# Two plain pairs instead of three at the head of each feed-forward part, and the token sums of two tiles moved ahead of the norm's root

## What is computed

```python
def _rmsnorm(x, g):
    r = xf * lax.rsqrt(jnp.mean(xf * xf, axis=-1, keepdims=True) + NORM_EPS)
    return r * g

def _swiglu(h, w_gate, w_up, w_down):
    return (jax.nn.silu(h @ w_gate) * (h @ w_up)) @ w_down

x = x + 1/2 * _swiglu(_rmsnorm(x, g), w_gate, w_up, w_down)     # D_FF = 2816
```

## Time and profile before

| | |
|---|---|
| median of 3 runs | 2819.61 us (2818.29 to 2819.61) |
| the profiled execution, its own time | 2818.11 us |
| its span, first to last instruction | 2815.9 us |
| TensorE busy | 2753.3 us, 98% |
| VectorE, ScalarE, GpSimd busy | 1442.4, 847.9, 1567.8 us |
| TensorE's mean granted clock | 0.993 |

### The profile page before, as it was taken

The page is one execution under the profiler, slowest core; times in us unless marked ns, Lnnn a source line. Parts: engine busy times, 40 slices in busy tenths (PEclk is TensorE's granted clock), DMA queues, the critical chain, the costliest instruction groups (busy, mean ns, idle before and its releaser), DMA issues.

```text
span 2815.9 us, 39727 instructions
## 1 busy us (share of the span) xinstructions
PE 2753.3 (98%) x14496; PEld 2306.6 (82%) x14496; DVE 1442.4 (51%) x1499; ACT 847.9 (30%) x1291; POOL 1567.8 (56%) x914
## 2 busy tenths in 40 slices
PE   7999999999999999999999999999999999999998
PEld 5888888888888888878988987887888888888886
DVE  7554554153556524027787866541447555553243
ACT  5333332132001112025656641111424333332222
POOL 3878775555454456645556554433044878774552
PEclk9999999999999999999999999999999999999999
DMA  3212224453222224322212113321021222224442
GB/s 134 105 67 89 89 82 157 156 210 127 105 89 97 105 98 154 125 91 71 55 35 56 50 52 127 114 78 42 0 97 68 93 79 89 73 84 174 176 157 104
DMA packets 125482, 278.36 MB, mean 99 GB/s; under 512 B 16592, under 2 KB 58704, under 8 KB 125160
## 3 DMA queue, kind: packets, MB, share of 16 engines
q1 hardware_dynamic: 103248, 215.67, 22.7%
q10 hardware_dynamic: 22168, 61.79, 5.8%
HBM read 215.46 MB, written 61.93 MB: 99 GB/s over the span
## 4 chain that ended last, share of the span: by engine, by line
PE 85%; issue 7%; POOL 4%; DVE 3%; ACT 1%; ACTq 0%; POOLq 0%; DVEq 0%
PE G L880 17%; PE G L881 17%; PE G L882 17%; PE G L964 9%; PE G L965 9%; PE G L966 9%; PE G L1222 2%; PE G L1391 1%; POOL AL L748 1%; PE G L1414 1%; PE G L1119 1%; PE G L1125 1%; DVE ylo L2562 0%; POOL rkb L723 0%; POOL Ys L708 0%
## 5 line engine op out<-in xcount | busy, mean ns | idle before, releaser
L806 POOL TENSOR_TENSOR whi<-raw,zero 128x1024 fp32r<-128x1024 f32 x129 | 249.5, 1934 | 826.1 <-PE G L882 784.2
L880 PE MATMUL G<-hhi,whi 128*128 128x512 f32 x1072 | 421.1, 393 | 17.4 <-DVE hlo L2032 17.4
L882 PE MATMUL G<-hhi,wlo 128*128 128x512 f32 x1072 | 418.6, 391 | 0.0
L881 PE MATMUL G<-hlo,whi 128*128 128x512 f32 x1072 | 418.6, 390 | 0.0
L809 POOL TENSOR_TENSOR wlo<-raw,whi 128x1024 fp32r<-128x1024 f32 x129 | 395.9, 3069 | 10.1
L2180 DVE TENSOR_TENSOR dl<-draw,dh 128x2048 fp32r<-128x2048 f32 x44 | 109.2, 2482 | 281.8 <-ACT dh L1639 281.8
L880 PEld LDWEIGHTS G<-hhi,whi 128*128 128x128 f32 x1072 | 202.0, 188 | 61.5 <-issue 15.4
L880 PE MATMUL G<-dh,whi 128*128 128x512 f32 x640 | 249.2, 389 | 0.0
L881 PE MATMUL G<-dl,whi 128*128 128x512 f32 x640 | 249.2, 389 | 0.0
L882 PE MATMUL G<-dh,wlo 128*128 128x512 f32 x640 | 249.2, 389 | 0.0
L882 PEld LDWEIGHTS G<-hhi,wlo 128*128 128x128 f32 x1072 | 202.0, 188 | 42.2
(11 more groups left out here) (443 smaller groups left out, 6507.1 us busy)
## 6 DMA issues: line engine op xcount, KB each, us to landing
draw<-a_d SPq DMA_DIRECT2D x44, 1024.0 KB, 5.8
a_d<-s SPq DMA_DIRECT2D x44, 512.0 KB, 3.0
raw<-in_wd SPq DMA_DIRECT2D x44, 512.0 KB, 3.5
raw<-in_wg SPq DMA_DIRECT2D x26, 512.0 KB, 3.9
raw<-in_wu SPq DMA_DIRECT2D x26, 512.0 KB, 4.8
raw_b<-in_wg SPq DMA_DIRECT2D x36, 256.0 KB, 3.4
raw_b<-in_wu SPq DMA_DIRECT2D x36, 256.0 KB, 4.1
x_park<-xT ACTq DMA_DIRECT2D x16, 512.0 KB, 2.6
```

The source lines that it names most:

```text
L806: nc.gpsimd.tensor_tensor(hi, raw[:, k, 0:w], zero[:].to_broadcast([P, w]), ALU.add).then_inc(hi_made, 1)
L880: nc.tensor.matmul(dst, wh, hi, start=start, stop=False)
L881: nc.tensor.matmul(dst, wh, lo, start=False, stop=False)
L882: return nc.tensor.matmul(dst, wl, hi, start=False, stop=stop)
```

## The change

`PLAIN` becomes 2 and `FAST` 20 in both feed-forward parts. VectorE's order becomes tile 0, tile 1, root, gate 0, tile 2, up 0, tile 3, gate 1, up 1. ScalarE's order becomes scale 0, scale 1, high 0, scale 2, high 1, scale 3, root, silu 0, high 2, weights' high parts 1 to 5 of fast pair 0, high 3, silu 1, high parts 6 and 7. The root's scratch (`nt_a`, `nms_a`) moves to a place that the token sums don't overwrite. As 20 is even, the peeled pair now stands in the loop's second place (`raw_b`, banks G2 and G3), the down product starts its tiles in the order 0 to 3, and one padding count of the bank semaphores goes.

```diff
-PLAIN = 3
+PLAIN = 2
 FAST = FFC - PLAIN
-PLAIN_AT = (1, 45)
+PLAIN_AT = (1, 43)
...
-    nt_a, nms_a = inside("x", 6 * ROW, "nt_a", [P, T]), inside("x", 7 * ROW, "nms_a", [P, T])
+    nt_a = nc.alloc_sbuf_tensor_at("nt_a", [P, T], F32, offset=sums_at - 12288)
+    nms_a = nc.alloc_sbuf_tensor_at("nms_a", [P, T], F32, offset=sums_at - 6144)
...
# SyncE
-            for u in range(2 * PLAIN - 1):
+            for u in range(2 * PLAIN):
                 plain(u)
+            sp.wait_ge(split_made, u0 + 2 * PLAIN + credit)
+            pair(0, 0)
             sp.wait_ge(dve_free, free + 1)
             store_a(0)
-            plain(2 * PLAIN - 1)
-            sp.wait_ge(split_made, u0 + 2 * PLAIN + credit)
-            pair(0, 0)
             sp.wait_ge(dve_free, free + 2)
             store_a(1)
             sp.wait_ge(unit_used, u0 + 2 * PLAIN + credit)
             pair(1, 1)
-            sp.wait_ge(dve_free, free + 3)
-            store_a(2)
...
# TensorE
-                    for o in (2, 3, 0, 1) if free is first_free else range(4):
+                    for o in range(4):
...
-            fast_pair(FAST - 1, 0, k, held[0])
-            c.advance(unit=2 * FAST, act=1, dve=1)
+            c.advance(unit=2 * FAST)
...
# ScalarE
         def ffn(own, gain, hi, nms, park=False):
-            norm_root(nms, nrf[:])
             k = c.unit % 2
             act.wait_ge(*nh_dve.at("l1", c.norm - 1))
...
             scale_tile(0, own)
-            plain_silu(0)
             scale_tile(1, own)
             tile_hi(0)
             scale_tile(2, own)
             tile_hi(1)
-            plain_silu(1)
             scale_tile(3, own)
+            norm_root(nms, nrf[:])
+            plain_silu(0)
             tile_hi(2)
-            tile_hi(3)
             c.advance(unit=2 * PLAIN)
             act.wait_ge(unit_used, c.unit - 1 + credit)
             for n in range(1, 6):
                 weight_hi(0, 0, n, k)
-            plain_silu(2)
+            tile_hi(3)
+            plain_silu(1)
             act.wait_ge(unit_used, c.unit + credit)
             for n in range(6, 8):
                 weight_hi(0, 0, n, k)
...
# VectorE
         def ffn(gain, hi, lo, nt, nms, nt_next, loads):
+            tile_sums(0)
+            tile_sums(1)
             norm_root(T, nms, nrf[:], nt)
             plain_gate(0)
-            tile_sums(0)
+            tile_sums(2)
             plain_up(0)
-            tile_sums(1)
+            tile_sums(3)
             plain_gate(1)
-            tile_sums(2)
             plain_up(1)
-            tile_sums(3)
-            plain_gate(2)
-            plain_up(2)
```

More of the change, by code:

```diff
@@ L599, in ffn_up @@
             pair(1, 1)
-            sp.wait_ge(dve_free, free + 3)
-            store_a(2)
-            with sp.Fori(1, FAST // 2) as i:
+            with sp.Fori(1, FAST // 2 - 1) as i:
                 for s in range(2):
@@ L607, in ffn_up @@
                     store_a(q + (PLAIN - 2))
-            pair(FAST - 1, 0)
+            pair(FAST - 2, 0)
+            sp.wait_ge(*st_dve.at("a1", c.fast + FAST - 4))
+            store_a(FAST - 4 + PLAIN)
+            pair(FAST - 1, 1)
             sp.wait_ge(a_out, (c.ffn * FFC + FFC - 3) * 16)
@@ L824, in _ @@
                         weight_sums(i * 2 + s, s, u0)
-                weight_sums(FAST - 1, 0, u0)
                 continue
@@ L1022, in first_free @@
             def first_free(o):
-                if o == 2:
+                if o == 0:
                     pe.wait_ge(*st_dve.at("c21", c.fast + FAST - 2))
-                elif o < 2:
-                    pe.wait_ge(*st_dve.at("c21" if o else "U3", c.fast + FAST - 1))
+                elif o >= 2:
+                    pe.wait_ge(*st_dve.at("c21" if o == 3 else "U3", c.fast + FAST - 1))
             def second_free(o):
@@ L1627, in ffn @@
                 weight_hi(0, 0, n, k)
-            c.advance(act=PLAIN + 1, dve=PLAIN + 1, a=PLAIN)
+            c.advance(act=PLAIN, dve=PLAIN, a=PLAIN)
             first = c.unit + 2 * FAST
@@ L1639, in down @@
                 activation(dh[v % 2][:], (draw[v % 2] if not isinstance(at, int) or at else draw0)[:], ACT.Copy).then_inc(*d_act.sig("hi"))
-            with act.Fori(0, FAST // 2) as i:
+            with act.Fori(0, FAST // 2 - 1) as i:
                 for s in range(2):
                     fast_pair(i * 2 + s, s, k)
-            fast_pair(FAST - 1, 0, k, False, down)
+            fast_pair(FAST - 2, 0, k)
+            fast_pair(FAST - 1, 1, k, False, down)
             c.advance(unit=2 * FAST)
@@ L2160, in ffn @@
             plain_gate(0)
-            tile_sums(0)
+            tile_sums(2)
             plain_up(0)
-            tile_sums(1)
+            tile_sums(3)
             plain_gate(1)
-            tile_sums(2)
             plain_up(1)
-            tile_sums(3)
-            plain_gate(2)
-            plain_up(2)
[L2170 to L2174, removed]
+            c.advance(unit=2 * PLAIN, act=PLAIN, dve=PLAIN, a=PLAIN)
             base = c.ffn * 2 * FFK
@@ L2180, in down @@
                 tt(dl[v % 2][:], src[:], dh[v % 2][:].bitcast(F32), ALU.subtract).then_inc(*d_dve.sig("lo"))
-            with dve.Fori(0, FAST // 2) as i:
+            with dve.Fori(0, FAST // 2 - 1) as i:
                 for s in range(2):
                     fast_pair(i * 2 + s, s)
-            fast_pair(FAST - 1, 0, lambda: down(0, 0))
+            fast_pair(FAST - 2, 0)
+            fast_pair(FAST - 1, 1, lambda: down(0, 0))
             c.advance(unit=2 * FAST)
```

## The result

The changed kernel takes 2838.96 us, median of 4 runs (2838.07 to 2839.65), against 2819.24 for the kernel before (2818.29 to 2819.61, 4 runs). The ratio is 1.0072, 95% interval [1.0056, 1.0088]: slower. The profiled execution's own time is 2838.07 us, its span 2835.7 us, 19.8 more than that of the kernel before. Here rows of the kernel after answer to those of before.

A forecast was written before the change was run, and what follows sets the result against it. TensorE, busy for 98% of the span, bounds the kernel, and loses whatever it waits for VectorE's chain. Heads and clock, 11.5 + 7.4 + 4 = +22.9 on 2818.1, give 2841; with 1.5 to the median, 2842 us (2827 to 2850).

The forecast's parts named there:

- Gain in matmuls: In each feed-forward part, a fast pair (19.3) replacing a plain pair (21.8) gains 2.5 us, plus 0.2 of waiting.
- First head: VectorE's chain to gate 1, counted with queueing behind GpSimd, starts fast pair 0 at 81.0; cost +11.5 us.
- Second head: The same chain count in the second head ends gate 1 at 2173.7; cost +7.4 us.
- That the root's operations queue: The root's three VectorE operations were assumed to wait behind GpSimd; if not, each head is some 2.4 us shorter.
- The clock: TensorE, idle for 10 us ahead of fast pair 0, then runs slower: 2 us per head, +4 in all, bounds 0 and 5.2.
- Edits at nothing: SP's later weight loads, the scratch's new place and the peeled last pair were costed at nothing.
- The count for SP and the late weights: In fast pair 0, block product 5's evacuation is done at about +14, and TensorE wants it at +13.8: level.
- The condition: If the slow clock's cover of 2 is gone, fast pair 1's late weights cost up to 1 us in each head.
- The sum: Both heads and the clock: 11.5 + 7.4 + 4 = +22.9 us on the profiled execution's 2818.1, giving 2841.
- Rival A: VectorE keeps up: fast pair 0 starts within 2.7 us of its natural time; at best 2814; chance 0.05.
- B: Queueing is half of that counted: fast pair 0 at 74 and 2169, +10.2 us, 2830; chance 0.15.
- C: Each tile costs what it did before: gate 1 ends at 83.7 and 2176.9, +29.8 us, 2849; chance 0.17.

The follow-up runs named there:

- e1: The kernel before, still with three plain pairs, given only the change's ScalarE and VectorE order and the scratch's new place; 2820.88 us.
- e4: The changed kernel with 28 idle matmuls into a free bank ahead of fast pair 0 in each head; 2840.45 us.
- e6: The changed kernel with the high parts of units 2 and 3 made by ScalarE in place of GpSimd in both heads; 2834.94 us.
- e5: The changed kernel with most of GpSimd's work in the first head cut to 32 columns, leaving out most of those weights' parts; 2826.26 us.
- e9: e5 with GpSimd's split of units 2 and 3 cut to 32 columns in the second head too; 2819.96 us.
- e3: The changed kernel with gate 1 evacuated ahead of tile 3's sums, up 1 behind them; 2845.61 us.
- e7: e3 with SP loading fast pair 1's weights ahead of the store of chunk 1; 2833.39 us.
- e8: The changed kernel with the edits of e6 and e7 together; 2831.44 us.

## Why the prediction was right

The forecast was 2842 (2827 to 2850), slower; the median is 2838.96. Step by step:

- **Gain in matmuls, 2.5 for each part.** The page has the 24 matmuls fewer, and a fast pair still takes 19.3 (85.92 to 105.23). Right.
- **First head.** Fast pair 0 at 81.0 was forecast and started at 80.79: +11.3 for +11.5. Within the chain, tile 0 ended at 41.8 (41.5), tile 1 at 50.9 (50.8), the root at 58.9 (60.4), tile 2 at 69.8 (70.4), up 0 at 73.3 (74.0), tile 3 at 79.4 (80.2). Only one of the root's three operations was held (2.17 where 1.23 is its pace), by 0.9 and not 2.3. Tile 2 made up half of that, 9.5 for the 8.8 counted. How many are held changes from trace to trace: one in e1 (2.80), two in e4 (2.22 and 2.17), none in e6. So agreement to a few tenths is in part luck. (The root's terms as written add up to 57.9 and not 58.1.)
- **Second head.** In before's time it started at 2184.46 - 10.35 = 2174.1, forecast 2173.7: +7.8 for +7.4. Here the root's first operation was held by the split of unit 3 for 2.1 (3.35).
- **That the root's operations queue** was the open bound. The runs show both sides: 3.35 beside a full split, 1.23 beside a narrow one (e5, e9).
- **The clock, 2 for each head.** From the first fast matmul to `s1c` it took 5.1 and 4.6 in place of 3.2 and 3.1 (the earlier trace rows and the rows of the second head above): 2.0 and 1.5. e4 measured the same 2.0 by removing it. The mechanism is shown, but that the size came out near 2 is in part luck: behind the long waits of e3 and e5 to e9 it was 1.4 to 2.5. Of the two rows that the 2 was taken from, the one at the kernel's start has 12 matmuls in 5.3 us, but a granted clock of 1.00; its 2.5 rests on the matmuls' pace alone.
- **Edits at nothing.** The count for SP and the late weights held: `s5c` came 13.8 after the first fast matmul (forecast 14), level with TensorE. The condition held too: where the slow clock was gone (e4, e5), it cost 1.0 to 1.1 (in e9's first head 0.5). The scratch and the peeled pair show no wait of their own in any of these profiles.
- **The sum.** Heads: 11.3 + 2.0 + 7.8 + 1.5 = 22.6 against 22.9. In the profile, the 2.9 by which the total is smaller is the middle. No trace shows why the median of the other runs is also 3 below the forecast; sixteen runs of the kernel before in a later session lie from 2812.75 to 2820.52, and I had no term for such scatter.

Rival A (VectorE keeps up) needed a GpSimd that isn't in the way. e5 is that case, and it only draws level in its head. B (half the queueing) is refuted by the first three tiles' 8.7, 9.1 and 9.5, and by 80.79 where it had 74. C (each tile as before) would have had gate 1 end at 83.7; it ended at 80.5. The queueing is told apart from both by e5 and e9: with GpSimd's operations cut and nothing taken from VectorE, the loss goes.

My reasons failed in the experiments. For e3 I had named the late weights in the prediction and then moved up 1 behind tile 3 without carrying the count through SP's queue, and I left out that gate 1 waits for the store of `s`. For e4 I did not count that the idle matmuls themselves start behind a rest. For e6 and e8 I took two GpSimd operations off the chain and left out that an earlier chain meets the next ones.

## What to carry to other kernels

Before taking covering work away from the engine that is the bound, write out the chain of the engine that was covered, with every operation of GpSimd that falls into it. An operation with two SBUF inputs is to be priced by what GpSimd does at that moment, not by its mean. When one wait is shortened, carry the count through to the next: the slow clock had hidden late weights, and the gate had hidden a store. To save 2.5 us of matmuls, a slack of the same size was all that this order had, and the chain missed it by 11.

## What the runs showed of the hardware

- GpSimd and VectorE wait for each other by whole operations, in turns, and GpSimd is held too: its split's first operation took 2.23 beside tile 1 and 1.89 where it started first. At 32 columns the two operations took 0.24 and 0.25 in e5's first head, and 0.88 and 1.20 in e9's second, beside VectorE's operations of 128x1024. One 128x512 sum of VectorE takes 0.60 alone, 1.7 to 1.8 beside a 128x512 operation, and up to 2.9 beside one of 128x1024. The Trainium skill (SBUF — State Buffer, "SBUF: two separate sides") says that the shared pair of ports is an exclusive lock, held for a whole instruction; the trace agrees, with the 3.35 and 1.23 of the same instruction in e5 and e9.
- I had not expected so short a rest to cost the clock. A rest of 3.6 us in e1, of 3.8 in e4 and of 4.3 in e9 brought TensorE to 1.2 GHz, and in e1 the loss behind the 3.6 was 2.9: the wait cost nearly twice its length. The length of the rest alone doesn't decide. A rest of 2.9 ahead of up 1 left the granted clock at 1.00 in the kernel after, but 0.61 and 0.66 followed the same rest in e3 and e7, and rests of 2.7 and 2.4 inside e3's fast pairs were followed by some 8 slow matmuls each. The rests of 1.7 (e5, e9) left it up.
- Nor does a longer rest cost more. From the first fast matmul to `s1c`, 3.15 at full speed, it took 5.6 behind a rest of 4.3 (e9), 4.8 behind 8.3 and 5.6 behind 7.0 (both e8), and 4.5 behind 10.3 (e5).
- The stretch between the heads took 2025.3 to 2030.1 us in eleven profiled executions. A difference of 3 us between two traces has to be shown at landmarks on both sides of the change before it is explained.
